# Adding the experts' results to the residual rows in memory by accumulating scatters

## The chip, the core and the metric

The kernel runs on one core of a Trainium2 chip. A core has a matrix engine (TensorE, PE in the profile), a vector engine (VectorE, DVE), a scalar engine (ScalarE, ACT), GpSimd (POOL) and a synchronising engine (SyncE, SP) that here only issues DMAs. Sixteen DMA engines move data between the device's memory and the core's on-chip memory. The metric is the device time of one execution in microseconds; less is better.

## What is computed

One layer of a decoder for 512 tokens of width 1024, all in float32: a norm, an input projection, two parallel token mixers, an output projection with a residual sum, and then a mixture of experts, which takes most of the time. Cut to what matters here:

```python
x = x + mix @ w_out[l]
h = rmsnorm(x, g_ffn[l])
# moe: softmax router, each token goes to the 4 best of 32 experts, gates g
#   expert e: act = clamped_swiglu(h[rows] @ w1[e] + b1[e])   w1[e]: 1024 x 2048
#             y   = act @ w2[e] + b2[e]                       w2[e]: 1024 x 1024
#   out[token] = sum over its 4 experts of g * y
x = x + moe(h, w_router[l], b_router[l], w1[l], b1[l], w2[l], b2[l])
return rmsnorm(x, g_final)
```

Every expert has 12.58 MB of weights, so all 32 have 403 MB, and each is read once.

## The kernel before

The engines run hand-written programs side by side and wait for one another on semaphores. The order of the work is thus the order in the code of each engine.

**Up to the router.** The mixers and the output projection come first. Then, for each of the four blocks of 128 tokens, VectorE writes the residual sum `X` (it stays on chip), `second_norm` makes the rows h, and ScalarE issues two stores of them: into `h2_dram`, which has four rows for each token (2048 rows of 4 KB), one store for the first copy and one for the other three (L1489, L1490). The router picks four experts for each token. VectorE computes where each of the 2048 pairs of token and expert stands in the experts' lists (`list_entries`, L1180). An entry has two numbers: the row 4 x token + k, where k is the rank of the expert among the token's four in order of work, and the gate. GpSimd scatters the entries into `slot_list` in memory (L1708), reads the lists back, and turns row numbers into numbers of half rows and quarter rows.

**Lists.** An expert's block has 64 slots whose rows are handled as two halves (128 lines of 2 KB). The 18 "big" experts have 32 slots more, handled in quarters (128 lines of 1 KB). `KINDS` gives the order of big and small: BBSS and then four times BBSBSBS. A slot without a token holds `UNUSED`, a number beyond the last row; the indirect DMAs have a bound, and a line whose index is beyond it is left out (`oob_is_err=False`).

**The expert stage.** `expert_blocks` calls the same step on each engine for expert i = 0 to 31. SyncE (`load`, L428) streams the weights through a ring of 16 slots of 1 MB: eight slots of w1 for expert i, four of w2 for expert i - 1, each load as soon as TensorE has used the slot (`slot_used`). TensorE (`compute`, L831) does w1 of expert i, turns the gathered rows of expert i + 1, does w2 of expert i - 1. VectorE and ScalarE do the activation, and ScalarE's `gated` (L1522) multiplies the result by the gates into `gated_y`, one of two buffers. GpSimd (`move`, L1724) issues, in this order: the scatter of expert i - 2, the gather of the rows of expert i + 2 once TensorE has turned the block before, and a small copy that selects the biases. The scatter writes gated rows into `expert_rows` (`y_dram`, 2048 rows, every row written once) as halves (L1690) and for a big expert quarters (L1693).

**The end.** As w1 of the last expert is used up, SyncE starts to read `expert_rows` back: rows k = 0, 1, 2 of all tokens, each set as soon as the scatters allow (a row k of some token can come from no expert after 28 + k in the order), and k = 3 after all scatters (`all_scattered`, L1771). VectorE adds each set to `X` (`add_row`, L1274). Then ScalarE squares and sums, VectorE multiplies by the reciprocal root and the gain (`last_norm`), and SyncE stores the output. The branches for overflowing experts are not taken with these inputs.

Of the kernel before, what the change touches and what calls it, by code (L numbers as in the profile page):

```python
# [5 lines left out]
F32 = mybir.dt.float32  # L6
# [4 lines left out]
ALU = mybir.AluOpType  # L11
# [3 lines left out]
P = 128  # L15
# [26 lines left out]
UNUSED = 1 << 20  # L42
ROWS = SEQ * TOPK
# [31 lines left out]
def layer_kernel(nc, x, g_mix, w_in, conv_w, sinks, g_attn_out, g_conv_out, w_out,  # L75
                 g_ffn, w_router, b_router, w1, b1, w2, b2, g_final, out):
    ctx = ExitStack()
    with ctx:
# [89 lines left out]
        first_row = sb("first_row", [P, TB])  # L168
        smaller = sb("smaller", [P, TB, TOPK, TOPK])
# [64 lines left out]
        h2_copies = h2_dram.rearrange("(t p k) n -> t p k n", p=P, k=TOPK)  # L234
# [52 lines left out]
        h2_turned, h2_stored, h2_copied = sem("h2_turned"), sem("h2_stored"), sem("h2_copied")  # L287
# [21 lines left out]
        yrow_in = [[sem(f"yrow{k}_in{t}") for t in range(TB)] for k in range(TOPK)]  # L309
        sum_ready, fstd_ready, fin_ready, out_written = sem("sum_ready"), sem("fstd_ready"), sem("fin_ready"), sem("out_written")  # L310
# [60 lines left out]
        def _(sp):  # L371
# [94 lines left out]
            n_ovf = overflow_count(sp)  # L466
            with sp.If(n_ovf < 1):
# [15 lines left out]
            def finish_overflow():  # L483
                sp.wait_ge(all_scattered, 1)
                for k in range(TOPK - 1):
                    load_row(k)

            overflow_blocks(sp, n_ovf, load_overflow, finish_overflow)

            sp.wait_ge(all_scattered, 1)
            load_row(TOPK - 1)
# [379 lines left out]
        def _(dve):  # L872
# [307 lines left out]
            def list_entries():  # L1180
# [20 lines left out]
                then(v.tensor_copy(row_i[:, :, :], row_f[:, :, :]))  # L1201
# [592 lines left out]
```

## Time and profile before

| | us |
|---|---|
| Median of 3 runs (lowest to highest) | 1254.84 (1253.53 to 1255.98) |
| The profiled execution | 1252.27 |
| its span in the trace | 1250.5 |
| TensorE busy | 1158.2 |
| VectorE busy | 309.7 |
| ScalarE busy | 198.1 |
| GpSimd busy | 169.9 |

The terms of an estimate come from the profiled execution and are summed against its own time; the median of the runs lies 2.6 us above it. Busy times overlap, and matmuls are pipelined, so a large busy time alone doesn't make an engine the bound. The share of the DMA engines and the waits have to be read beside it.

### The profile page before, as it was taken

Reading aid. Unit: us, or ns where it says so; the run is one execution under the profiler, and the core shown is the slowest. Engines: PE = TensorE matmul, PEld = TensorE weight load, DVE = VectorE, ACT = ScalarE, POOL = GpSimd, SP = SyncE. Lnnn points to the kernel's source line nnn. Section 1 sums busy time; section 2 is a strip of 40 time slices with the busy share of each in tenths; the row PEclk is TensorE's granted clock in tenths of the full one; section 3 lists DMA queues with packets and bytes.
Section 4 is the critical chain, followed back from the end, with each engine's and each line's share of the span. In section 5 each row is a group of like instructions: output and inputs, shape, how many; then the busy total and the mean of one; then the engine's idle time right before and its main releaser. Section 6 shows DMA issues by size and latency. Waiting matters only on the chain. (4 is left out here: it accounts for less than half of the span.)

```text
span 1250.5 us, 16597 instructions
## 1 busy us (share of the span) xinstructions
PE 1158.2 (93%) x7030; PEld 484.9 (39%) x7030; DVE 309.7 (25%) x470; ACT 198.1 (16%) x385; POOL 169.9 (14%) x246
## 2 busy tenths in 40 slices
PE   5999998798999999999999898999989899998980
PEld 4777677323333333333333333333333333333330
DVE  4678855411101202101101010110101011010108
ACT  4453623001001101011010000101000010100002
POOL 6000000341111201111111011111101111111000
PEclk9999989698999999999999999999999999999995
DMA  9400635999999999999999999999999999999996
GB/s 332 145 1 27 236 142 220 320 392 411 423 424 424 423 425 423 425 422 425 424 423 425 425 423 424 425 423 423 424 424 424 423 425 423 424 423 424 425 394 249
DMA packets 59246, 460.67 MB, mean 368 GB/s; under 512 B 12438, under 2 KB 12710, under 8 KB 26306
## 3 DMA queue, kind: packets, MB, share of 16 engines
q1 hardware_dynamic: 49362, 434.15, 84.0%
q0 software_dynamic: 7632, 17.05, 3.6%
q10 hardware_dynamic: 2176, 8.39, 1.7%
q8 instruction: 57, 0.93, 0.3%
q14 instruction: 19, 0.16, 0.0%
HBM read 442.58 MB, written 21.41 MB: 371 GB/s over the span
## 5 line engine op out<-in xcount | busy, mean ns | idle before, releaser
L778 PE MATMUL ps<-ring_a,blockT 128*64 128x512 f32 x1472 | 327.2, 595 | 15.6 <-DMA ring_a<-in_w 15.5
L1234 DVE TENSOR_SCALAR xnT<-ps 128x768 f32<-128x768 f32 (+1 forms) x32 | 26.9, 841 | 828.4 <-PE ps L785 520.6
L778 PEld LDWEIGHTS ps<-ring_a,blockT 128*64 128x64 f32 x1472 | 101.1, 137 | 226.8 <-issue 187.7
L804 PE MATMUL ps<-ring_a,actT 128*64 128x512 f32 x736 | 166.3, 598 | 0.0
L1497 ACT ACTIVATE blockT<-ps 128x512 f32<-128x512 f32 x30 | 17.9, 597 | 561.4 <-PE ps L730 561.4
L778 PE MATMUL ps<-ring_b,blockT 128*64 128x512 f32 x448 | 99.7, 595 | 6.7 <-DMA ring_b<-in_w 6.7
L1674 POOL DMA_INDIRECT scores<-h_rows,slots x30 | 31.7, 1058 | 509.6 <-PE ps L730 508.7
L785 PE MATMUL ps<-ring_a,blockT 128*32 128x512 f32 x768 | 87.4, 595 | 0.0
L804 PEld LDWEIGHTS ps<-ring_a,actT 128*64 128x64 f32 x736 | 50.2, 137 | 93.5 <-issue 91.0
L1690 POOL DMA_INDIRECT expert_rows<-normed,slots x32 | 32.9, 1029 | 270.1 <-ACT normed L1526 269.8
L804 PE MATMUL ps<-ring_b,actT 128*64 128x512 f32 x288 | 64.7, 596 | 0.0
L524 PE MATMUL ps<-xnT_hi,ring_r 128*128 128x512 f32 x144 | 57.8, 401 | 5.6 <-DVE ring_r L892 3.5
L778 PEld LDWEIGHTS ps<-ring_b,blockT 128*64 128x64 f32 x448 | 30.7, 137 | 71.0 <-issue 57.3
L525 PE MATMUL ps<-xnT_lo,ring_r 128*128 128x512 f32 x144 | 56.9, 395 | 0.0
L526 PE MATMUL ps<-xnT_hi,ring_r 128*128 128x512 f32 x144 | 56.8, 394 | 0.0
L810 PE MATMUL ps<-ring_a,actT 128*32 128x256 f32 x832 | 50.3, 382 | 0.0
L785 PEld LDWEIGHTS ps<-ring_a,blockT 128*32 128x32 f32 x768 | 22.5, 109 | 62.6 <-issue 62.6
L1255 DVE TENSOR_TENSOR xnT<-xnT 128x768 f32<-128x768 f32 (+1 forms) x32 | 42.7, 1334 | 9.3 <-ACT xnT L1520 8.7
L810 PEld LDWEIGHTS ps<-ring_a,actT 128*32 128x32 f32 x832 | 24.4, 109 | 34.5 <-issue 21.1
L1525 ACT ACTIVATE normed<-ps,slots 128x256 f32<-128x256 f32 x18 | 8.5, 474 | 174.5 <-PE ps L810 174.5
L1526 ACT ACTIVATE normed<-ps,slots 128x512 f32<-128x512 f32 x32 | 21.9, 684 | 81.8 <-PE ps L804 81.8
L804 PEld LDWEIGHTS ps<-ring_b,actT 128*64 128x64 f32 x288 | 20.0, 136 | 35.9 <-issue 35.0
(289 smaller groups left out, 1090.3 us busy)
## 6 DMA issues: line engine op xcount, KB each, us to landing
ring_a<-in_w SPq DMA_DIRECT2D x98, 2048.0 KB, 32.1
ring_a<-in_w SPq DMA_DIRECT2D x92, 1024.0 KB, 30.1
ring_b<-in_w SPq DMA_DIRECT2D x30, 2048.0 KB, 31.0
ring_b<-in_w SPq DMA_DIRECT2D x36, 1024.0 KB, 32.8
ring<-in_w_in SPq DMA_DIRECT2D x12, 768.0 KB, 19.2
ring<-expert_rows SPq DMA_DIRECT2D x16, 512.0 KB, 14.7
h_rows<-normed ACTq DMA_DIRECT2D x4, 1536.0 KB, 6.5
X<-in_x SPq DMA_DIRECT2D x8, 512.0 KB, 6.1
```

The costliest lines, as they stand in the source:

```text
L524: mm(ps[:, bank, :], high[:, k, :], xnT_hi[:, k, :], start=(k == 0), stop=False)
L525: mm(ps[:, bank, :], high[:, k, :], xnT_lo[:, :, k, :], start=False, stop=False)
L526: ins = mm(ps[:, bank, :], low[:, k, :], xnT_hi[:, k, :], start=False, stop=(k == KT - 1))
L778: ins = mm(ps[half * HALF:(half + 1) * HALF, b, :], x_of(k)[0], ring(r)[:, 0, at + half * 512:at + (half + 1) * 512], start=False, stop=(k ...
L785: mm(ps[q * QUARTER:(q + 1) * QUARTER, B_BOTH, :], x_of(k)[1], w[:, :, q * 256:(q + 1) * 256], start=False, stop=(k == KT - 1), tile_posit ...
L804: ins = mm(ps[half * HALF:(half + 1) * HALF, bank, :], actT[:, s % 2 * W2_K + j, s // 2 * HALF:(s // 2 + 1) * HALF], ring(r)[:, 0, j * D + ...
L810: ins = mm(ps[q * QUARTER:(q + 1) * QUARTER, bank + 1, 0:256], actT[:, 4 + j, s * QUARTER:(s + 1) * QUARTER], ring(slot(s)[0])[:, 0, j * D ...
L1234: v.tensor_scalar(width(glu_c, big), width(ps_glu, big), LIMIT, None, ALU.min).then_inc(glu_ready, 1)
L1255: v.tensor_tensor(turned.rearrange("p (s k q) -> p s q k", k=W2_K, q=P), a_in.rearrange("p (s q k) -> p s q k", k=W2_K, q=P), b_in.rearran ...
L1526: a.activation(gated_y[:, parity, 0:512], ps[:, bank, :], ACT.Copy, scale=gates[:, HALVES, 1:2].bitcast(F32)).then_inc(y_ready, 1)
L1674: g.indirect_dma_start(gathered[:, 0:512], None, h2_halves, bass.IndirectOffsetOnAxis(lists[:, HALVES, 0:1], 0), bounds_check=last_half_ro ...
L1690: g.indirect_dma_start(y_halves, bass.IndirectOffsetOnAxis(slots[:, HALVES, i, 0:1], 0), gated_y[:, parity, 0:512], None, bounds_check=las ...
```

## The change

The results are no longer kept as four rows for each token. ScalarE stores the residual rows `X` to memory too (`x2_rows`, 512 rows and 640 spare rows behind them), and every expert's scatter adds its gated rows to them with an accumulating indirect DMA. The sum is read back once, into `X`. From this follow:

- `h2_dram` has one row for each token; one store of 0.5 MB instead of 2 MB, and one of 0.5 MB for `X`.
- An entry names the token instead of 4 x token + k, so the operations that found k go, and `entry` is filled by GpSimd beforehand.
- An unused entry holds 512 + its rank in the list, a spare row of `x2_rows`: the gather still leaves it out, the scatter adds something to a spare row.
- A token may be in the lists of several experts, so a scatter first waits until the scatter of the expert before has landed (`y_out[1 - parity]`).
- At the end 4 reads of 0.5 MB instead of 16, and no additions on VectorE.

```diff
-        h2_dram = nc.dram_tensor("h2_rows", (ROWS, D), F32).ap()
+        h2_dram = nc.dram_tensor("h2_rows", (SEQ, D), F32).ap()
-        y_dram = nc.dram_tensor("expert_rows", (ROWS, D), F32).ap()
+        x2_dram = nc.dram_tensor("x2_rows", (SEQ + LIST_RANKS, D), F32).ap()
...
@@ SyncE, the end
-            y_dram_v = y_dram.rearrange("(t p k) n -> k p t n", p=P, k=TOPK)
-
-            def load_row(k):
-
-                for t in range(TB):
-                    sp.dma_start(y_rows[:, k, t, :], y_dram_v[k][:, t, :]).then_inc(yrow_in[k][t], 16)
...
-                for k in range(TOPK - 1):
-                    sp.wait_ge(slot_used, USES * (w1_slot(E - 1, KT - 1) + 1))
-                    for b in range(2):
-                        sp.wait_ge(y_out[b], scatters(b, E - TOPK + k))
-                    load_row(k)
...
             sp.wait_ge(all_scattered, 1)
-            load_row(TOPK - 1)
+            for t in range(TB):
+                sp.dma_start(X[:, t, :], x2_dram[t * P:(t + 1) * P, :]).then_inc(x_in[t], 16)
...
@@ VectorE, second_norm, list_entries and the end
-                    dve.wait_ge(h2_copied, 16 * t)
...
-                then(v.tensor_copy(row_i[:, :, :], row_f[:, :, :]))
-                then(v.tensor_tensor(picked[:, :, :, :].rearrange("p t k e -> p (t k) e"), onehot[:, :, :, :].rearrange("p t k e -> p (t k) e"),
-                                     by_place.to_broadcast([P, TB * TOPK, E]), ALU.mult))
-                then(v.tensor_reduce(row_f[:, :, :], picked[:, :, :, :], AX_X, ALU.add))
-                then(v.tensor_tensor(smaller[:, :, :, :], row_f[:, :, :].unsqueeze(3).to_broadcast([P, TB, TOPK, TOPK]),
-                                     row_f[:, :, :].unsqueeze(2).to_broadcast([P, TB, TOPK, TOPK]), ALU.is_gt))
-                then(v.tensor_reduce(row_f[:, :, :], smaller[:, :, :, :], AX_X, ALU.add))
-                v.tensor_tensor(entry[:, :, :, 0:1].rearrange("p t k w -> p t (k w)"), row_f[:, :, :], first_row[:, :].unsqueeze(2).to_broadcast([P, TB, TOPK]),
-                                ALU.add).then_inc(entries_ready, 1)
+                v.tensor_copy(row_i[:, :, :], row_f[:, :, :]).then_inc(entries_ready, 1)
...
-            def add_row(k, t):
-                dve.wait_ge(yrow_in[k][t], 16)
-                if k:
-                    dve.wait_ge(sum_ready, (k - 1) * TB + t + 1)
-                v.tensor_tensor(X[:, t, :], X[:, t, :], y_rows[:, k, t, :], ALU.add).then_inc(sum_ready, 1)
...
             for t in range(TB):
-                add_row(TOPK - 1, t)
-                dve.wait_ge(sum_ready, (TOPK - 1) * TB + t + 1)
-                if t:
-                    last_norm(t - 1)
-            last_norm(TB - 1)
+                last_norm(t)
...
@@ ScalarE, the stores and the end
-                act.dma_start(h2_copies[t, :, 0, :], normed[:, t % 2, :]).then_inc(h2_stored, 16)
-                act.dma_start(h2_copies[t, :, 1:TOPK, :], normed[:, t % 2, :].unsqueeze(1).to_broadcast([P, TOPK - 1, D])).then_inc(h2_copied, 16)
+                act.dma_start(h2_dram[t * P:(t + 1) * P, :], normed[:, t % 2, :]).then_inc(h2_stored, 16)
+                act.dma_start(x2_dram[t * P:(t + 1) * P, :], X[:, t, :]).then_inc(x2_stored, 16)
...
-                act.wait_ge(sum_ready, (TOPK - 1) * TB + t + 1)
+                act.wait_ge(x_in[t], 48)
...
@@ GpSimd, the spare rows and the scatters
-            then(g.memset(list_fill, UNUSED))
+            then(g.iota(list_fill.rearrange("p (b e) -> p b e", b=LIST_RANKS // P), [[1, LIST_RANKS // P], [0, 2 * E]], base=SEQ, channel_multiplier=LIST_RANKS // P))
...
+            def add_parts(lists, big, parity, done):
+
+                g.indirect_dma_start(x2_halves, bass.IndirectOffsetOnAxis(lists[:, HALVES, 0:1], 0), gated_y[:, parity, 0:512], None,
+                                     bounds_check=end_halves, oob_is_err=True, compute_op=ALU.add).then_inc(done, 16)
+                if big:
+                    g.indirect_dma_start(x2_quarters, bass.IndirectOffsetOnAxis(lists[:, QUARTERS, 0:1], 0), gated_y[:, parity, 512:768], None,
+                                         bounds_check=end_quarters, oob_is_err=True, compute_op=ALU.add).then_inc(done, 16)
+
             def scatter(i, parity):
                 pool.wait_ge(y_ready, i + 1)
-                g.indirect_dma_start(y_halves, bass.IndirectOffsetOnAxis(slots[:, HALVES, i, 0:1], 0), gated_y[:, parity, 0:512], None,
-                                     bounds_check=last_half_row, oob_is_err=False).then_inc(y_out[parity], 16)
...
+                if i:
+                    pool.wait_ge(y_out[1 - parity], scatters(1 - parity, i - 1))
+                add_parts(slots[:, 0:2, i, :], BIG[i], parity, y_out[parity])
...
-            pool.wait_ge(h2_copied, 16 * TB)
+            pool.wait_ge(x2_stored, 16 * TB)
```

On GpSimd the last scatters stand like this in the kernel before: expert 29, then 30 (two parts), then 31, and the read of the overflow count. `normed` is the buffer of the gated rows.

```order
L1648 COPY bias_sel<-expert_sel 96x128 [waits w2_begun]
L1690 DMA expert_rows<-normed,slots 4096x512 [waits y_ready] x2
L1693 DMA expert_rows<-normed,slots 8192x256
L1690 DMA expert_rows<-normed,slots 4096x512 [waits y_ready]
L358 TENSOR_LOAD ovf_row [waits ovf_in,y_out1,y_out0]
```

And like this in the changed kernel, where `x_rows` is the tensor of the residual rows:

```order
L1594 COPY bias_sel<-expert_sel 96x128 [waits w2_begun]
L1637 DMA x_rows<-normed,slots 2304x512 [waits y_out0,y_ready]
L1637 DMA x_rows<-normed,slots 2304x512 [waits y_out1,y_ready]
L1640 DMA x_rows<-normed,slots 4608x256
L1637 DMA x_rows<-normed,slots 2304x512 [waits y_out0,y_ready]
L352 TENSOR_LOAD ovf_row [waits ovf_in,y_out1,y_out0]
```

The scatters stand where they stood, and each has got a wait for the one before.

On VectorE the end of the kernel before has the last set of additions between the norms:

```order
L1278 TENSOR_TENSOR X<-X,ring 128x1024 x2
L1296 RECIPROCAL stat<-stat 128x1
L1298 SCALAR_TENSOR_TENSOR ring<-X,stat,gain_a 128x1024
L1278 TENSOR_TENSOR X<-X,ring 128x1024
L1296 RECIPROCAL stat<-stat 128x1
L1298 SCALAR_TENSOR_TENSOR ring<-X,stat,gain_a 128x1024
```

In the changed kernel only the norms are left:

```order
L356 UNCONDITIONAL_BRANCH
L1245 RECIPROCAL stat<-stat 128x1
L1247 SCALAR_TENSOR_TENSOR ring<-X,stat,gain_a 128x1024
L1245 RECIPROCAL stat<-stat 128x1
L1247 SCALAR_TENSOR_TENSOR ring<-X,stat,gain_a 128x1024
```

The four additions here and the twelve of the other sets ahead of them are gone.

## Rows read from the trace of the kernel before

**Rows 1.** The page: busy us (share) xinstructions; DMA busy in tenths, 40 slices of the span.

```profile
PE 1158.2 (93%) x7030; PEld 484.9 (39%) x7030; DVE 309.7 (25%) x470; ACT 198.1 (16%) x385; POOL 169.9 (14%) x246
...
DMA  9400635999999999999999999999999999999996
```

**Rows 2.** Stretches: us, busy us (instructions) of PE, PEld, DVE, ACT, POOL; PE clock, DMA share, GB/s.

```profile
235.00:300.00 65.00, 58.08 (x356) 18.83 (x356) 12.41 (x19) 5.20 (x8) 21.98 (x27) 0.92 1.01 391
...
385.00:594.00 209.00, 209.00 (x1338) 71.46 (x1336) 26.66 (x32) 20.93 (x41) 31.23 (x31) 1.00 1.01 424
594.00:812.00 218.00, 210.28 (x1334) 70.70 (x1332) 26.67 (x32) 20.87 (x40) 29.59 (x29) 1.00 1.01 424
```

**Rows 3.** Timeline of ScalarE: start us, us; sigmoids of three experts, each seven apart.

```profile
407.38 0.83 ACT L1520 ACTIVATE xnT<-xnT 128x768 f32<-128x768 f32 x1
...
615.88 0.83 ACT L1520 ACTIVATE xnT<-xnT 128x768 f32<-128x768 f32 x1
...
833.78 0.84 ACT L1520 ACTIVATE xnT<-xnT 128x768 f32<-128x768 f32 x1
```

**Rows 4.** Waits, whole span: engine line <- releaser: us in total, times, longest.

```profile
POOL scores L1674 <- PE ps L730: 508.7, 29, 21.9
...
PEld ps L778 <- DMA ring_a<-in_w: 36.8, 31, 2.7
...
DVE stat L1078 <- ACT stat L1322: 5.0, 4, 1.5
```

**Rows 5.** DMA issues: count, KB each, median us from issue to landing.

```profile
ring_a<-in_w SPq DMA_DIRECT2D x98, 2048.0 KB, 32.1
```

**Rows 6.** DMA queue of GpSimd, whole span: packets, MB, share of 16 engines.

```profile
q0 software_dynamic: 7632, 17.05, 3.6%
```

**Rows 7.** DMA queues from 300 to 1200 us: SyncE's, with the weights, and GpSimd's.

```profile
q1 hardware_dynamic: 33421, 364.94, 96.3%
q0 software_dynamic: 6288, 15.34, 4.4%
```

**Rows 8.** Timeline of the tail: start us, us, instruction, idle before it and its releaser.

```profile
1198.05 3.65 PE L778 MATMUL ps<-ring_a,blockT 128*64 128x512 f32 x16 [1.06 <-DMA ring_a<-in_w]
...
1216.82 0.98 POOL L1693 DMA_INDIRECT expert_rows<-normed,slots  x1 [0.30 <-issue]
...
1237.60 1.06 ACT L1568 ACTIVATE ring<-X 128x1024 f32<-128x1024 f32 x1 [13.39 <-DVE X L1278]
...
1238.98 1.04 ACT L1568 ACTIVATE ring<-X 128x1024 f32<-128x1024 f32 x1
```

**Rows 9.** The chain that ended last: start us, us, what.

```profile
1222.76 1.20 DMA expert_rows<-normed,slots
1223.96 6.05 issue
...
1231.38 4.88 DMA ring<-expert_rows
...
1246.19 1.29 DVE ring L1298
```

**Rows 10.** Scatters of halves (L1690), all 32, from issue to landing.

```profile
DMA to landing us min/median/max: 5.5/7.9/10.0
```

**Rows 11.** Timeline of GpSimd: two scatters and the gather between them.

```profile
331.27 1.03 POOL L1690 DMA_INDIRECT expert_rows<-normed,slots  x1 [9.95 <-ACT normed L1526]
...
345.75 1.06 POOL L1674 DMA_INDIRECT scores<-h_rows,slots  x1 [12.14 <-PE ps L730]
...
353.72 1.03 POOL L1690 DMA_INDIRECT expert_rows<-normed,slots  x1 [4.58 <-ACT normed L1526]
```

**Rows 12.** Timeline between the router and the first expert.

```profile
227.32 1.09 POOL L1683 DMA_INDIRECT scores<-h_rows,tok_static  x1 [74.34 <-DVE tok_static L1146]
...
236.81 0.69 DVE L1202 TENSOR_TENSOR scores<-scores,where 128x512 f32<-128x512 f32 x1
...
239.87 1.04 POOL L1708 DMA_INDIRECT slot_list<-entry,row_i  x1 [5.42 <-DVE entry L1208]
```

More of the change, by code:

```diff
@@ L41 @@
 NEG = -1e30
-UNUSED = 1 << 20
-ROWS = SEQ * TOPK
 LIST_BLOCKS = SEQ // P
@@ L307, in layer_kernel @@
         all_scattered = sem("all_scattered")
-        yrow_in = [[sem(f"yrow{k}_in{t}") for t in range(TB)] for k in range(TOPK)]
-        sum_ready, fstd_ready, fin_ready, out_written = sem("sum_ready"), sem("fstd_ready"), sem("fin_ready"), sem("out_written")
+        fstd_ready, fin_ready, out_written = sem("fstd_ready"), sem("fin_ready"), sem("out_written")
         dve_final, act_final = sem("dve_final"), sem("act_final")
@@ L481, in load_overflow @@
                     load_w2(e, k, KT + k)
[L483 to L488, printed above, removed]
+            overflow_blocks(sp, overflow_count(sp), load_overflow)
             sp.wait_ge(all_scattered, 1)
-            load_row(TOPK - 1)
+            for t in range(TB):
+                sp.dma_start(X[:, t, :], x2_dram[t * P:(t + 1) * P, :]).then_inc(x_in[t], 16)
             for t in range(TB):
@@ L1266, in _ @@
             expert_blocks(elementwise)
-            def add_rows():
-                for k in range(TOPK - 1):
-                    for t in range(TB):
-                        add_row(k, t)
-            def add_row(k, t):
-                dve.wait_ge(yrow_in[k][t], 16)
-                if k:
-                    dve.wait_ge(sum_ready, (k - 1) * TB + t + 1)
-                v.tensor_tensor(X[:, t, :], X[:, t, :], y_rows[:, k, t, :], ALU.add).then_inc(sum_ready, 1)
-            n_ovf = overflow_count(dve)
-            with dve.If(n_ovf < 1):
-                add_rows()
             def overflow(o, i):
@@ L1287, in overflow @@
                 activated(i, True)
-            overflow_blocks(dve, n_ovf, overflow, add_rows)
+            overflow_blocks(dve, overflow_count(dve), overflow)
             dve.wait_ge(gfinal_in, 16)
@@ L1619, in _ @@
             g.iota(iota_o[:, :], [[0, 1]], base=0, channel_multiplier=1, allow_small_or_imprecise_dtypes=True)
-            g.iota(first_row[:, :], [[P * TOPK, TB]], base=0, channel_multiplier=TOPK, allow_small_or_imprecise_dtypes=True)
-            g.iota(tok_value[:, :, 0:1], [[0, TB], [0, 1]], base=0, channel_multiplier=TOPK, allow_small_or_imprecise_dtypes=True)
-            g.iota(tok_value[:, :, 1:2], [[P * TOPK, TB], [0, 1]], base=-16384, channel_multiplier=0, allow_small_or_imprecise_dtypes=True)
+            for t in range(TB):
+                g.iota(entry[:, t, :, 0:1], [[0, TOPK], [0, 1]], base=t * P, channel_multiplier=1)
+            g.iota(tok_value[:, :, 0:1], [[0, TB], [0, 1]], base=0, channel_multiplier=1, allow_small_or_imprecise_dtypes=True)
+            g.iota(tok_value[:, :, 1:2], [[P, TB], [0, 1]], base=-16384, channel_multiplier=0, allow_small_or_imprecise_dtypes=True)
             g.iota(expert_no[:, :], [[0, 1]], base=0, channel_multiplier=1, allow_small_or_imprecise_dtypes=True)
@@ L1661, in _ @@
             g.iota(iota_r[:, 0:HALF].rearrange("p (a b) -> p a b", b=8), [[1, 8], [8, 8]], base=-1024, channel_multiplier=0, allow_small_or_imprecise_dtypes=True).then_inc(consts_ready, 1)
-            last_row = pool.to_reg(ROWS - 1)
-            last_half_row = pool.to_reg(2 * ROWS - 1)
-            last_quarter_row = pool.to_reg(4 * ROWS - 1)
+            last_row = pool.to_reg(SEQ - 1)
+            last_half_row = pool.to_reg(2 * SEQ - 1)
+            last_quarter_row = pool.to_reg(4 * SEQ - 1)
             h2_halves = h2_dram.rearrange("t (h n) -> (t h) n", h=2)
             h2_quarters = h2_dram.rearrange("t (h n) -> (t h) n", h=4)
-            y_halves = y_dram.rearrange("t (h n) -> (t h) n", h=2)
-            y_quarters = y_dram.rearrange("t (h n) -> (t h) n", h=4)
+            x2_halves = x2_dram.rearrange("t (h n) -> (t h) n", h=2)
+            x2_quarters = x2_dram.rearrange("t (h n) -> (t h) n", h=4)
+            end_halves, end_quarters = (pool.to_reg(n * (SEQ + LIST_RANKS) - 1) for n in (2, 4))
             list_rows = list_dram.rearrange("(r e) w -> r (e w)", e=E)
```

15 lines of the change are left out of this document (2 added, 13 removed).

## The prediction

> **What bounds the kernel now.** I read the share of each engine first [rows 1]: TensorE is busy 93% of the span, which looks like the bound. The same page has the 16 DMA engines at 9 tenths or more in 32 of the 33 slices from the eighth on [rows 1]. Two resources are nearly full, so the question is which one sets the pace. The table by stretches [rows 2] shows DMA at 1.01 of its time and 424 GB/s from 385 us to 812 us, whatever TensorE does. TensorE is busy without a gap from 385 to 594 us, then 210.3 of 218 us. The sigmoids, seven experts apart [rows 3], give the two periods: 615.88 - 407.38 = 208.5 us while TensorE still lives on weights that were loaded ahead, then 833.78 - 615.88 = 217.9 us once that lead is used up. So TensorE needs 29.8 us for an expert and DMA 31.1 us. A check from bytes: seven experts are 7 x 12.58 MB of weights plus 7/32 of 16.78 MB gathered and scattered, 91.8 MB; at 424 GB/s that is 216 us, the measured period. TensorE's waits for weights are short and many [rows 4], and a weight load takes some 30 us to land although 2 MB at 424 GB/s need 5 [rows 5]: the queue always holds most of the ring. Hence **DMA is the bound from about 235 us to about 1198 us**, and every microsecond of DMA engine time added there is a microsecond of span.
>
> After the last w1 tile lands (TensorE resumes with it at 1198.05 us [rows 8]) comes a tail without slack: TensorE's last products, the last scatter, the read of the last of four row sets, the final norm [rows 8, 9].
>
> **1. The scatters: bytes.** Before, list entries without a token lie outside the bounds and move nothing. The software queue shows it: 17.05 MB [rows 6] are two times 8.39 MB (2048 rows of 4 KB, gathered and scattered) and 0.27 MB of lists. The gathers stay so. The scatters do not: an unused entry now names a spare row behind the 512 tokens, so all lines move. A big expert moves 128 x 2 KB + 128 x 1 KB = 393 KB, a small one 262 KB; 18 big and 14 small make 10.75 MB instead of 8.39. Before the last w1 load has landed experts 0 to 29 are scattered: 17 x 0.393 + 13 x 0.262 = 10.09 MB now, against 30/32 x 8.39 = 7.86 MB before.
>
> **2. The scatters: price.** Between 300 and 1200 us the software queue moved 15.34 MB in 4.4% of 16 engines' 900 us, 39.6 us: 387 GB/s; the weights' queue 364.94 MB in 866.7 us, 421 GB/s [rows 7]. The old scatters cost 7.86 / 387 = 20.3 us. No row shows an accumulating DMA. The lower bound is what a plain scatter of its bytes costs: 10.09 / 387 = 26.1 us, **+5.8 us**. The upper is a gather and a scatter of its bytes, since it must fetch the old row as a gather does and pass the new one as a scatter does: 52.1 us, **+31.8 us**. I take the upper, because the nearest rows say that an engine's time goes by what it takes in: gathers, scatters and weights, of either direction, all add up to one 1.01 and one 424 GB/s [rows 2, 7], so a second operand that has to be taken in should not be free. A gain is excluded here: more bytes, and nothing is taken from this stage.
>
> The Trainium skill, in "Collectives: The Full Stack", section "The bandwidth ceiling: the fold count and why AG ≠ RS ≠ AR", says of the sum in a DMA engine that the addition itself costs nothing but that it needs two reads on the same ring, and that this halves the rate. By that rule the step is the upper value, +31.8 us; without it, from 1.01 of plain copies alone, the lower, +5.8 us, can't be excluded. No run here shows it yet.
>
> **3. The new wait.** Each scatter now waits on GpSimd for the one before it to land. Queued behind it are the gather of rows for the next-but-one expert and the copy of the bias selector. Scatters land in a median of 7.9 us, at most 10.0 [rows 10]; the closest two are 22.4 us apart (331.27 and 353.72), and the gather behind them waits another 14.5 us for TensorE (345.75) [rows 11]. In all, GpSimd waits 508.7 us for TensorE before its gathers [rows 4]. Cost 0, as long as landing stays under 22 us; beyond some 30 us it would starve TensorE of rows.
>
> **4. The stored copies of h.** Instead of 2 MB per 128 tokens, 0.5 MB of h and 0.5 MB of x. All of it stands before 235 us. VectorE's second norm, which also waits for the copies, was released by ScalarE all four times [rows 4]. The last store competes with weights at 216 us, but the first gather is issued at 227.32 us, released by VectorE's static list and not by a store [rows 12]. Gain 0, at most 0.5 us.
>
> **5. Five VectorE operations fewer for the list.** The first starts at 236.81 us, and GpSimd's first list scatter, which waits for the last, at 239.87: 3.1 us, of which the 0.9 of a release stay, so about 2 [rows 12]. The first indexed gather comes earlier by that. But DMA is at 1.01 in this stretch too [rows 2], so TensorE only gains lead. Worth 0. If TensorE were the bound it would be worth 2 us.
>
> **6. The tail.** Fewer row reads (6 MB less, two thirds of them beside TensorE's last products), no additions, one more wait.
> - Scatter 30's second part is issued at 1216.82 [rows 8]. With a landing of some 7.4 us (a little under the median of all, since the row reads that competed are gone) plus 1 to 2 us for the accumulation it lands at about 1225.5; scatter 31, which started at 1222.76, starts 2.7 us later. It needed 7.25 us to 1230.01 [rows 9]; in an emptier queue the smallest landing of all is 5.5 us [rows 10], plus 1 to 2 for the accumulation, so 7 again. SP is released at about 1234 instead of 1231.38: +2.6 us.
> - Before, from there: 4.88 us to the first row's landing, then for each 128 tokens an addition and a norm on VectorE; the last norm ends at 1246.19 + 1.29 = 1247.48, 16.1 us after the issue [rows 9]. Now ScalarE squares what landed: 4.9 us, four steps of 1.38 us (1238.98 - 1237.60 [rows 8]), the last root 0.3, reciprocal 0.2, norm 1.29 [rows 9], gaps 0.1: 12.4 us. The gain is 3.7 us; the 3.0 us of the last store stay.
> - Sum of the tail: -3.7 + 2.6 = **-1.1 us**. At best (landing 5.5 us twice, no wait) -5.6 us; at worst, with landings of 12 us, +7 us.
>
> **Sum.** The profiled execution took 1252.27 us (span 1250.5). 1252.27 + 31.8 - 1.1 = 1283.0 us. It lies 2.6 us under the median of the runs, 1254.84, on which the same sum gives 1285.5; I say **1285 us**. A measurement of this kernel can tell some 0.2% (2.5 us) from no change.
>
> **Rivals.**
> - *One pass.* The old row is fetched beside the other traffic and only the extra lines cost: +5.8 - 1.1, 1259.5 us; half way to the forecast 1272. For it: reading and writing could overlap in an engine. Against: traffic of both directions did not make the mixed queues faster than weights alone.
> - *Faster: the weight stream is not touched and the tail is shorter.* Place: the last 30 us. If an engine adds in the shade of the packets of weights, steps 1 and 2 cost 0 and the best tail holds: 1254.84 - 5.6 = 1249 us. It decides when the added DMA time of 30 scatters is below about 1 us. Against: 1.01 busy everywhere [rows 2] and 2.2 MB more, 5.3 us at 424 GB/s.
> - *Accumulation is slower than its bytes.* Each line of 1 or 2 KB waits in the engine for its old value. At twice my price, 104.2 - 20.3 - 1.1 = +82.8, 1338 us; above 22 us of landing the wait of step 3 joins in. For it: lines are small and nothing in the trace shows such a DMA. Against: a landing of 7.9 us for 8 or 16 lines per engine beside a queue of weights shows that plain lines at least are handled one behind another without stalls.
> - *No difference:* price near 1 pass and the best tail: 1254.84 + 5.8 - 5.6 = 1255 us.
>
> **Chances.** Forecast (1275 to 1297): 0.50. One pass or between (1257.5 to 1275): 0.22. Slower than its bytes (above 1297): 0.18, half of it below 1322. Within 0.2%: 0.06. Faster: 0.04. A range of 1258 to 1322 leaves out the last two, the other half of the third, and little else: 2 in 10. Slower 0.90, same 0.06, faster 0.04.
>
> **What would show it.** Right: seven experts take about 225 us (218 + 7 x 31.8/30) with DMA still at 1.01; TensorE's waits for w1 in the ring's first part grow from 36.8 us [rows 4] to above 55; the software queue's share rises from 3.6% [rows 6] to about 6%; scatters land in 9 to 13 us; the last norm ends 12 us after SP's first read. Wrong: a period of 218 to 219.5 us (one pass or none); landings above 20 us with GpSimd waiting for the scatter before (the slow rival); DMA share below 1 with TensorE without gaps, which would mean that the bound was misread.

## The result, and the profile after

| | before | changed |
|---|---|---|
| Median of 4 runs each, us | 1255.41 | 1273.86 |
| lowest to highest | 1253.53 to 1257.28 | 1272.39 to 1276.39 |
| Profiled execution / its span | 1252.27 / 1250.5 | 1274.83 / 1273.0 |
| Ratio, 95% interval | | 1.0149, 1.0134 to 1.0164 |

The change costs 18.5 us, 1.5%. The forecast was 30, with 1258 to 1322 as the range: right in sign and cause, and too large by 12 us.

The queues from 300 to 1200 us (packets, MB, share of 16 engines), of the changed kernel, answer to [rows 7]:

```profile
q1 hardware_dynamic: 32298, 353.10, 93.2%
q0 software_dynamic: 9696, 17.22, 8.2%
```

GpSimd's queue takes 8.2% of the engines' time instead of 4.4%, 34 us more in 900, while its bytes rose only from 15.34 to 17.22 MB. The weights' queue still moves 421 GB/s while it is served, but it is served 93.2% of the time and not 96.3%, so in the same 900 us it has delivered 12 MB less, nearly an expert's weights. The 3.1% that the weights' queue lost are 28 us. The bytes counted for the whole span show that the old value that an accumulating line fetches isn't counted:

```profile
q0 software_dynamic: 11408, 19.40, 6.7%
```

19.40 MB are 8.39 (gathers) + 10.75 (all lines) + 0.27 (lists). Against [rows 6] this is the 2.36 MB of unused lines and nothing else.

The sigmoids of the same three experts as in [rows 3], and that of the last expert, in ScalarE's timeline of the changed kernel:

```profile
409.37 0.83 ACT L1465 ACTIVATE xnT<-xnT 128x768 f32<-128x768 f32 x1
...
625.62 0.84 ACT L1465 ACTIVATE xnT<-xnT 128x768 f32<-128x768 f32 x1
...
850.83 0.83 ACT L1465 ACTIVATE xnT<-xnT 128x768 f32<-128x768 f32 x1
...
1231.63 0.63 ACT L1465 ACTIVATE xnT<-xnT 128x512 f32<-128x512 f32 x1 [18.76 <-DVE xnT L1199]
```

Seven experts take 850.83 - 625.62 = 225.2 us where they took 217.9. In the seven before them the lead of loaded weights ran out earlier: 216.3 us instead of 208.5. The last sigmoid is a good mark between stream and tail, since everything behind it is bound to the end and not to the weights: in nine of the fourteen traces of this document the last scatter starts 20.25 us after it, whatever the kernel. In the kernel before it stood here:

```profile
1202.50 0.63 ACT L1520 ACTIVATE xnT<-xnT 128x512 f32<-128x512 f32 x1 [17.33 <-DVE xnT L1234]
```

So in this pair of traces the stream got 29.1 us longer, and the tail behind the mark went from 1250.5 - 1202.5 = 48.0 to 1273.0 - 1231.6 = 41.4 us. TensorE's waits for weights say the same (compare the first with [rows 4]; columns us in total, times, longest):

```profile
PEld ps L752 <- DMA ring_a<-in_w: 57.4, 40, 3.4
...
PEld ps L752 <- DMA ring_b<-in_w: 18.7, 12, 3.4
...
POOL x_rows L1637 <- DMA x_rows<-normed,slots: 5.2, 1, 5.2
```

The last of these rows is the new wait: of 31 scatters that could have waited for the one before, one did, the last (in e6's trace below, with the same wait, none did). An accumulating scatter of halves lands later in the stream than a plain one in [rows 10], and sooner at the end:

```profile
L1637 POOL DMA_INDIRECT x_rows<-normed,slots x32: 1571/1629/1657, 306.1 to 1253.3; - x32
...
DMA to landing us min/median/max: 4.8/11.6/12.6
```

The first row also shows GpSimd needing 1.63 us to issue one, where the plain one took 1.03 [rows 11].

The end of the chain (start us, us, what), against [rows 9]:

```profile
1253.29 1.57 DMA x_rows<-normed,slots
1254.86 3.35 issue
...
1259.26 3.40 DMA X<-x_rows
...
1268.63 1.28 DVE ring L1247
```

From the last scatter's start to SP's read it takes 5.97 us (8.62 before), from there to the end of the last norm 10.65 us (16.1 before).

### The profile page after: what moved, and what is told of

The parts are those of the page before. It is cut to its first block and busy times, and to the rows that moved or that the text cites. A ratio compares the mean times of both kernels' runs of the same rounds, so it can differ in the third digit from the quotient of the medians.

```text
span 1273.0 us, 16579 instructions
## 1 busy us (share of the span) xinstructions
PE 1171.3 (92%) x7030; PEld 484.6 (38%) x7030; DVE 287.6 (23%) x449; ACT 197.8 (16%) x385; POOL 200.6 (16%) x249
## 3 DMA queue, kind: packets, MB, share of 16 engines
q0 software_dynamic: 11408, 19.40, 6.7%
HBM read 436.29 MB, written 17.22 MB: 356 GB/s over the span
## 5 line engine op out<-in xcount | busy, mean ns | idle before, releaser
L752 PE MATMUL ps<-ring_a,blockT 128*64 128x512 f32 x1472 | 336.6, 606 | 26.3 <-DMA ring_a<-in_w 25.7
L752 PE MATMUL ps<-ring_b,blockT 128*64 128x512 f32 x448 | 103.9, 613 | 9.4 <-DMA ring_b<-in_w 9.2
L1637 POOL DMA_INDIRECT x_rows<-normed,slots x32 | 51.8, 1618 | 271.8 <-ACT normed L1471 266.3
L759 PEld LDWEIGHTS ps<-ring_a,blockT 128*32 128x32 f32 x768 | 22.5, 109 | 62.6 <-issue 62.6
```

What stands on the lines that cost most here:

```text
L752: ins = mm(ps[half * HALF:(half + 1) * HALF, b, :], x_of(k)[0], ring(r)[:, 0, at + half * 512:at + (half + 1) * 512], start=False, stop=(k ...
L759: mm(ps[q * QUARTER:(q + 1) * QUARTER, B_BOTH, :], x_of(k)[1], w[:, :, q * 256:(q + 1) * 256], start=False, stop=(k == KT - 1), tile_posit ...
L1637: g.indirect_dma_start(x2_halves, bass.IndirectOffsetOnAxis(lists[:, HALVES, 0:1], 0), gated_y[:, parity, 0:512], None, bounds_check=end_h ...
```

## The experiments

Below, "stream" is the time of the last sigmoid in the profiled execution, "tail" the span behind it. "From expert 3" is the part of the stream behind the sigmoid of expert 3: that sigmoid stands anywhere from 344.7 to 349.9 us in the fourteen traces, without order by kernel (346.27 and 349.87 us in the two of the kernel before), and this is no effect of the scatters. Medians are of runs beside runs of the kernel before on the same chip, and each ratio is against those: their medians were 1256.04 us for e1 to e4, 1254.16 us for e5 to e8 and 1255.93 us for e9 to e12.

| kernel | median, us | ratio (95%) | stream | from expert 3 | tail |
|---|---|---|---|---|---|
| before | 1255.41 | 1 | 1202.5 | 856.2 | 48.0 |
| changed | 1273.86 | 1.0149 (1.0134 to 1.0164) | 1231.6 | 883.4 | 41.4 |
| e1 plain, all lines | 1248.33 | 0.9946 (0.9931 to 0.9960) | 1207.7 | 859.2 | 38.4 |
| e2 adding, used lines | 1268.30 | 1.0092 (1.0077 to 1.0107) | 1226.1 | 877.9 | 40.3 |
| e3 plain, used lines | 1244.22 | 0.9903 (0.9889 to 0.9917) | 1203.4 | 857.2 | 38.4 |
| e4 adding, half width | 1248.91 | 0.9938 (0.9925 to 0.9950) | 1206.0 | 860.6 | 38.0 |
| e5 three reads back | 1283.38 | 1.0214 (1.0187 to 1.0242) | 1234.2 | 885.0 | 48.7 |
| e6 four additions back | 1276.01 | 1.0176 (1.0150 to 1.0202) | 1229.7 | 884.3 | 44.0 |
| e7 two sums, no wait | 1274.13 (one run) | | 1232.2 | 884.8 | 40.1 |
| e8 before again | 1258.06 (one run) | | 1207.6 | 857.7 | 48.6 |
| e9 gather beside scatter | 1267.61 | 1.0089 (1.0071 to 1.0107) | 1225.6 | 879.8 | 38.4 |
| e10 before, slots spread | 1252.01 | 0.9970 (0.9958 to 0.9982) | 1200.5 | 853.9 | 47.7 |
| e11 e2, slots spread | 1260.41 | 1.0040 (1.0026 to 1.0054) | 1218.0 | 873.3 | 39.9 |
| e12 copies of h back | 1274.21 | 1.0145 (1.0124 to 1.0166) | 1230.8 | 885.2 | 40.6 |

### e1, e2, e3: addition and unused lines, each alone

```diff
@@ e1 and e3 (both calls in add_parts)
-                                     bounds_check=end_halves, oob_is_err=True, compute_op=ALU.add).then_inc(done, 16)
+                                     bounds_check=end_halves, oob_is_err=True).then_inc(done, 16)
@@ e2 and e3
-                                     bounds_check=end_halves, oob_is_err=True
+                                     bounds_check=last_half_row, oob_is_err=False
... (the quarters likewise)
```

> The changed kernel with a plain indirect write in place of the accumulating one; all lines are still moved, the unused ones into the spare rows. The sum over experts is left out (the last writer of a row stands). Theory A (an accumulating line costs an engine two passes, a plain one a single pass): the scatters of experts 0 to 29 cost 26 us instead of 50 to 52, so the last w1 load lands 5 to 6 us later than in the kernel before, the tail is about 6 us shorter as in the changed kernel, and the time is that of the kernel before within 2 us, some 19 us under the changed one. Theory B (the stretch comes from the spare lines or from the wait for the scatter before, not from the addition): 1268 to 1274 us, as in the changed kernel. Landing of a scatter: A 8 to 9 us, B 12 us.

> The changed kernel with the unused lines left out of the accumulating scatters by the bound, as in the kernel before; the addition stays. Theory A (time goes by bytes, two passes each): 7.86 MB twice at 387 GB/s are 40.6 us against 20.3 before, so the last w1 load lands 20 us later than before and 9 us earlier than in the changed kernel: about 1264 us. Theory B (the lines cost, whether they carry a used slot or not): no difference from the changed kernel, 1272 to 1275 us.

> The changed kernel with plain writes and with unused lines left out: the scatters' traffic is that of the kernel before, and only the new end (one set of rows read, no additions), the smaller stores and the shorter list are left of the change. The sum over experts is left out. Theory A: the last w1 load lands as in the kernel before within 1.5 us, and the whole gain of the tail shows, 5 to 7 us under the kernel before: 1249 to 1250 us. Theory B (the tail gains 1 us, as the working of the prediction had it): 1254 us.

With plain writes the whole loss is gone, and e1 is 7 us under the kernel before; with the unused lines left out too, what is left of the change is a gain of 12 us (e3). e3's stream is that of the kernel before (from expert 3, 857.2 us against 856.2 and 857.7); its tail is 9.6 us shorter. The addition costs 24.1 us on the used lines (e2 less e3), of which 1.9 in the tail. The unused lines cost 4.1 us by the medians and 5.4 by the ratios when written plainly (e1 less e3), and 5.6 or 7.2 when added (changed less e2): under the 5.8 and well under the 11.5 us that one and two passes over 2.23 MB would take. e2 itself came out 4 us above what theory A had for it. e1 came out some 7 us and e3 5 us under their figures; 3 to 4 us of that are the tail, which gained more than I had put in, and the rest was not traced. The bytes set the sign and the rough size, and something else a part of it; e10 and e11 ask for that.

### e4: bytes or lines

```diff
-        x2_dram = nc.dram_tensor("x2_rows", (SEQ + LIST_RANKS, D), F32).ap()
+        x2_dram = nc.dram_tensor("x2_rows", (SEQ + LIST_RANKS, D // 2), F32).ap()
... (the store of x and the last read take half the columns too)
@@ add_parts: the halves; the quarters, [:, parity, 512:768], become [:, parity, 512:640]
-gated_y[:, parity, 0:512], None,
+gated_y[:, parity, 0:256], None,
```

> The changed kernel with residual rows of half the width: every accumulating line carries half its bytes (1 KB and 512 B), with the same number of lines. The right half of the columns is left out of the experts' sum, and the last read is half as long. Theory A (price by bytes): half of the scatters' 52 us stays, 26 us, so 5 to 6 us above the kernel before in the stream, and 7 to 9 us less in the tail: 1251 to 1255 us. Theory B (price by lines, each waiting for its old value): nearly the whole 29 us of the stream stays, less some 2 us in the tail: 1268 to 1272 us.

1248.9 us, 2 us under theory A's range and far from theory B's. With as many accumulating lines of half the length the stream ends at 1206.0 us, next to e1's 1207.7: two passes of half lines against one pass of full ones, the same number of bytes. Halving the bytes took the stream's excess over e3 from some 27 us to 3.4 (from expert 3), since half of two passes is the one that e3 pays too. The price goes by bytes, two passes of them; a line that waits in the engine for its old value is ruled out as the main term. The queue's row of e4 from 300 to 1200 us, and that of e1:

```profile
q0 software_dynamic: 9840, 12.44, 5.8%
```

```profile
q0 software_dynamic: 6294, 17.48, 4.9%
```

The share is a little larger in e4 though the stream isn't longer, so the share of an accumulating queue reads high: what it adds to the busy time is not all taken from the weights.

### e9: is an addition a gather and a scatter?

```diff
             def scatter(i, parity):
                 pool.wait_ge(y_ready, i + 1)
+                if i < E - 2:
+                    read_old(i)
...
@@ read_old (halves; quarters likewise; each expert's waits for the one before)
+                g.indirect_dma_start(upper[:, 0:512], None, h2_halves, bass.IndirectOffsetOnAxis(slots[:, HALVES, i, 0:1], 0),
+                                     bounds_check=last_half_row, oob_is_err=False).then_inc(old_in, 16)
```

> The kernel of e3 (plain scatters of the used lines, new end, the sum over experts left out), and for experts 0 to 29 a plain gather of the same lines (of h, into a spare tile) is issued just ahead of the scatter. That is what step 2 of the prediction took an accumulating scatter to be. Theory A (the price of the addition is the pass that fetches the old row): 7.86 MB at 387 GB/s, +20 us on e3's 1244.2 us, 1264 us, which is e2 (1268.3 us) less 2 us of its longer tail and within 3 us. Theory B (an accumulating line costs more than a gather and a scatter): 1254 to 1260 us. Theory C (it costs less): above 1268 us.

1267.61 us, +23.4 us on e3; e2, with the addition, +24.1 us. The streams end at 1225.6 and 1226.1 us. Of the 1.9 us by which e2's tail is longer, 1.6 lie between the start of its last scatter and SP's read (5.92 us against 4.33), and 0.3 in that read. The figure of theory A was 3.6 us too low, because a pass cost 23.4 us and not 20 (e10 and e11 are about that), but its comparison with e2 holds. That is the prediction's price of step 2 shown directly: for the weight stream, an accumulating scatter costs what a gather and a scatter of its lines cost, within 1 to 2 us of 23 (from expert 3, e9 is 1.9 us longer than e2).

### e5, e6, e7: the tail

```diff
@@ e5, SyncE, where the kernel before had its reads
+            for k in range(TOPK - 1):
+                sp.wait_ge(slot_used, USES * (w1_slot(E - 1, KT - 1) + 1))
+                for b in range(2):
+                    sp.wait_ge(y_out[b], scatters(b, E - TOPK + k))
+                for t in range(TB):
+                    sp.dma_start(y_rows[:, k + 1, t, :], old_v[k][:, t, :]).then_inc(yrow_in[k][t], 16)
@@ e6, VectorE
+                v.tensor_tensor(X[:, t, :], X[:, t, :], gain_a[:, :], ALU.add).then_inc(sum_ready, 1)
@@ e7, GpSimd (and a second tensor, x2_odd, for odd experts)
-                if i:
-                    pool.wait_ge(y_out[1 - parity], scatters(1 - parity, i - 1))
+                if i >= 2:
+                    pool.wait_ge(y_out[parity], scatters(parity, i - 2))
```

> The changed kernel, and beside it the three further sets of 2 MB are read at the end at the points where the kernel before read rows k = 0, 1, 2 (from other memory; nothing is added from them, so the result is the changed kernel's). Theory A (the tail got shorter because nothing competes with the last scatter and the last read): from the start of the last scatter to SP's release it takes 8 to 9 us again instead of 6.0, the last scatter also starts some 1 to 3 us later since the one before lands later, and the time rises by 4 to 7 us. Theory B (the reads were hidden beside TensorE's last products anyway, as the prediction had it for two thirds of them): at most 2 us.

> The changed kernel with one VectorE addition of 128x1024 put back for each block of tokens between the last read and the norm, as in the kernel before. What is added is a constant tile, so the output is off by it. Theory A (additions and norms take turns on VectorE, 2.7 us for a block instead of 1.4): the end of the last norm comes 4 to 5 us after that of the changed kernel, +4 to +5 us. Theory B (the reads set the pace and additions hide in it): +1.5 us.

> The changed kernel with two tensors for the sum, one for even and one for odd experts, so that no scatter waits for the one before it (only for the one before that). The odd tensor is left out of the final sum. Theory A (in the stream the wait costs nothing, in the tail it costs what the landing of scatter 30 takes): w1's last tile is used within 1.5 us of the changed kernel's time, the last scatter starts 24.7 us after that instead of 26.1. Theory B (the wait holds GpSimd and the gathers behind it): the stream gets 10 us shorter or more.

The tail falls into four parts, us, from the profiled executions:

| kernel | mark to start of last scatter | to SP's read | to its first landing | to the end | tail |
|---|---|---|---|---|---|
| before | 20.3 | 8.6 | 4.9 | 14.2 | 48.0 |
| e8 before again | 20.5 | 9.0 | 4.9 | 14.2 | 48.6 |
| e3 plain, used lines | 20.3 | 4.4 | 3.4 | 10.3 | 38.4 |
| changed | 21.7 | 6.0 | 3.4 | 10.3 | 41.4 |
| e12 copies of h back | 21.0 | 5.9 | 3.4 | 10.3 | 40.6 |
| e5 three reads back | 24.7 | 10.3 | 3.4 | 10.3 | 48.7 |
| e6 four additions back | 20.3 | 6.1 | 3.4 | 14.3 | 44.0 |
| e7 two sums, no wait | 20.3 | 5.9 | 3.5 | 10.3 | 40.1 |

e5's tail is 48.7 us, 7.3 more than the changed kernel's. GpSimd's timeline shows where the first part goes:

```profile
1249.09 1.56 POOL L1653 DMA_INDIRECT x_rows<-normed,slots  x1 [0.30 <-issue]
1258.88 1.57 POOL L1650 DMA_INDIRECT x_rows<-normed,slots  x1 [8.23 <-DMA x_rows<-normed,slots]
```

The last scatter waits 8.23 us for the one before (5.18 in the changed kernel), and the chain shows the second part: it lands late, beside the third set, whose reads land from 1263.60 to 1269.26 us.

```profile
1258.88 1.57 DMA x_rows<-normed,slots
1260.45 7.69 issue
...
1269.20 3.39 DMA X<-x_rows
```

10.3 us from its start to SP's read instead of 6.0. Theory A holds, above its upper figure by the medians (+0.65%, 8 us). In the changed kernel such reads would be paid twice, in the wait for the scatter before and in the last landing. The kernel before has no such wait, and its last scatter starts 20.3 us after the mark like e3's. Its price for the reads is read against e3, whose end is this:

```profile
1223.62 0.98 DMA x_rows<-normed,slots
...
1228.01 3.44 DMA X<-x_rows
```

From the last scatter's start to SP's read e3 takes 4.4 us, the kernel before 8.6, and its first read 4.9 instead of 3.4, since three of its third set's reads land only after that read is issued (at 1232.47 to 1234.98 us, against 1231.38). So there the reads cost 5.7 us. They were not hidden. e5 doesn't repeat the slower first read: there the third set has landed when it starts.

e6's tail is only 2.6 us longer than the changed kernel's, but its last scatter happened to start 1.4 us earlier after the mark, as the table shows. Behind the first landing it takes 14.3 us instead of 10.3, 3.9 us more, and the last norm ends 14.6 us after SP's read instead of 10.65: the 4 to 5 us of theory A, at their lower end (by the ratios the time rises by 3.4 us). The kernel before has the same 14.2 us. The start of e6's chain, and four pieces from it that show VectorE's norm of one block followed at once by the addition of a later one:

```profile
1249.94 1.57 DMA x_rows<-normed,slots
...
1256.03 3.42 DMA X<-x_rows
...
1265.22 1.29 DVE ring L1248
1266.51 1.15 DVE X L1253
...
1267.68 1.16 ACT ring L1519 x2
...
1269.39 1.28 DVE ring L1248
```

e7's stream ends at 1232.2 us, as the changed kernel's within 0.6, and its tail is 1.3 us shorter. Here the last scatter starts when ScalarE has written its rows:

```profile
1252.47 1.57 POOL L1640 DMA_INDIRECT x_odd<-normed,slots  x1 [3.78 <-ACT normed L1472]
```

That is 24.7 us after the last w1 tile is used, theory A's figure. So the wait costs nothing in the stream. At the end it cost 1.4 us in the changed kernel's trace, 0.7 in e12's and nothing in e6's, which all have it. Between e3 and the kernel before the pieces close: 38.4 us, with 5.7 for the reads and 3.9 for the additions, are 48.0. The changed kernel keeps of that 1.4 us of wait and 1.6 us of slower landing.

### e8: the kernel before, a second time

> The kernel before, unchanged, profiled a second time, since its first profiled execution lay 2.6 us under the median of its runs. Theory A (what varies between its executions is the tail, where its row reads and the last scatter compete): the last w1 tile is used within 1 us of 1198 us and the rest takes 1 to 4 us longer than 52.4 us. Theory B (the weight stream varies): the last w1 tile comes 1 to 4 us later, the tail takes 52 to 53 us.

The tail is nearly the same (48.6 us), the stream ends 5.1 us later: theory B, a little above its figures. Most of the 5.1 us stands already in the first experts, while TensorE still has its lead. The sigmoid of expert 2, in the first and the second trace (e8):

```profile
318.93 0.62 ACT L1520 ACTIVATE xnT<-xnT 128x512 f32<-128x512 f32 x1
```

```profile
322.53 0.62 ACT L1520 ACTIVATE xnT<-xnT 128x512 f32<-128x512 f32 x1
```

3.6 us of 5.1. The two traces lie on either side of the kernel's median (1252.27 and 1258.06 against 1255.41 us), and the changed kernel's 1.0 us above its own, which is why the pair of profiles shows 22.5 us where the medians show 18.5. What varies there was not looked into.

### e12: the stores of h

```diff
+                act.dma_start(h2_more.rearrange("(t p k) n -> t p k n", p=P, k=TOPK - 1)[t], normed[:, t % 2, :].unsqueeze(1).to_broadcast([P, TOPK - 1, D])).then_inc(x2_stored, 16)
@@ GpSimd
-            pool.wait_ge(x2_stored, 16 * TB)
+            pool.wait_ge(x2_stored, 32 * TB)
@@ VectorE, second_norm
+                    dve.wait_ge(x2_stored, 32 * t)
```

> The changed kernel with the three further copies of h stored again for each block of tokens (into a tensor that nobody reads), and with the waits on them where they were. Theory A (step 4 of the prediction: all this lies before the weight stream is the bound): within 1 us of the changed kernel, 1272 to 1275 us. Theory B (6.3 MB less to store is a gain hidden in the total): 1277 us or more, and the first w1 product of expert 0 starts 2 us later or more.

No difference (ratios 1.0145 and 1.0149): 6.3 MB of stores ahead of the stream are free.

### e10, e11: where the unused lines stand

```diff
@@ list_entries
-                v.tensor_scalar(eighths.bitcast(I32), moved.bitcast(I32), 3, None, ALU.logical_shift_right)
+                v.tensor_scalar(eighths.bitcast(I32), moved.bitcast(I32), 4, None, ALU.logical_shift_right)
...
-                v.scalar_tensor_tensor(out=eighths, in0=moved, scalar=-9.0, in1=ranks[:, :, :], op0=ALU.mult, op1=ALU.add)
+                v.scalar_tensor_tensor(out=eighths, in0=moved, scalar=-21.0, in1=ranks[:, :, :], op0=ALU.mult, op1=ALU.add)
...
-                then(v.scalar_tensor_tensor(out=moved, in0=moved, scalar=7.0, in1=ranks[:, :, :], op0=ALU.mult, op1=ALU.add))
+                then(v.scalar_tensor_tensor(out=moved, in0=moved, scalar=3.0, in1=ranks[:, :, :], op0=ALU.mult, op1=ALU.add))
```

The quarters and the two lists that are made ahead (`iota_r`) follow in the same way; four lines more.

> The kernel before, with another order of the slots within a block: rank r of a list goes to line 4r - 63 floor(r/16) of the halves instead of 8r - 63 floor(r/8), and likewise in the quarters, so that used lines are spread over groups of four neighbouring lines from the first 16 ranks on. Reason: in e1, e2, e3 and the changed kernel the unused lines cost 4.1 us when written plainly and about 5 us when accumulated, where their bytes at 387 GB/s would be 5.8 and 11.5 us. 
> The kernel of e2 (accumulating scatters of the used lines only) with the slot order of e10. Theory A: gathers once and accumulating scatters twice, so 3 x 48 KB x 16 at 387 GB/s, 6 us under e2's 1268.3: 1262 us. Theory B: as e2. In both, still some 7 us or more above the kernel before, since the second pass remains.

Both came as theory A has it: the kernel before gains 3.9 us (ratio 0.9970, 0.9958 to 0.9982; 4 expected), e2 gains 7.9 us by the medians and 6.5 by the ratios (6 expected). Neither moves a byte more or less, as the rows for 300 to 1200 us show, e10's first, with 15.34 MB as in [rows 7], and e11's 15.15 MB, which e2 has too:

```profile
q0 software_dynamic: 6288, 15.34, 4.4%
```

```profile
q0 software_dynamic: 9696, 15.15, 6.9%
```

So where the left-out lines stand counts, and not the bytes alone. That it is the fullest group of lines that sets the cost is what theory A says; both sizes agree with it, but no row shows a single DMA engine, and the new order also changes the order in which rows of memory are visited; the two were not separated. e10 leaves nothing of the computation out and is faster than both kernels. e11 is the best form of the accumulating scatters found here, and still 0.4% slower than the kernel before: the second pass outweighs the tail.

## Why the prediction was right, and where it was off

**The bound.** Right. DMA was at 1.02 of its time in the changed kernel and the added pass lengthened the period of seven experts. The forecast period was 225 us, the measured one 225.2.

**Step 1, bytes.** Right for the queue (19.40 MB). Wrong as a measure of the old price: 7.86 MB with lines left out did not cost 7.86 MB. Theory A of e10 and e11 counts lines by the DMA engine that moves them; by the counts of these inputs the fullest engine then carried 588 KB in each direction where the mean was 512 and all lines are 656. (The assignment of lines to engines is that of the Trainium skill, "DMA: Bandwidth & Descriptors", "The descriptor swizzle"; e10 and e11 bear it out by their effect, and no trace here shows it.) For 30 of 32 scatters that is 9.0 MB worth, 23.3 us, and by this estimate the change adds 28.8 instead of 31.8 us. The same count gives e9 less e3 as 23.3 us (measured 23.4), e2 less e3 as 23.3 + 1.9 (24.1), and the changed kernel less e2 as 5.5 (5.6).

**Step 2, price.** The mechanism and the end of the range that was taken were right: e9 equals e2, e4 excludes a price by lines, e1 fits one pass. The Trainium skill's rule on reductions ("Collectives: The Full Stack", "The bandwidth ceiling: the fold count and why AG ≠ RS ≠ AR"), that the addition is free and the second read is not, agrees with e2, e4 and e9. One caution goes with it: the queue's own busy share overstates the loss, 34 us of share against some 27 us of stream (and 28 us of share that the weights' queue lost).

**The stream's total.** The changed kernel and its four relatives with the same scatters (e5, e6, e7, e12) end their streams at 1229.7 to 1234.2 us, 1231.7 on average; the kernel before at 1202.5 and 1207.6. That is 27 us with an uncertainty of some 3, against 31.8. Counted from expert 3, where the spread between executions falls out, it is 883.4 to 885.2 us against 856.2 and 857.7: 27.6 us. The corrected count explains 3.0 of the difference. Where the rest is was not tested. The sigmoids of experts 3 to 8 stand 2.0 us later in this pair of traces, all alike, but in e6 and e12, which have the same scatters, they stand up to 0.9 us earlier than before, so that shift says nothing on the scatters.

**Step 3, the wait.** Right for the stream: nothing (e7). The closest two scatters are 22.4 us apart only there; in the tail scatter 31 starts 5.9 us behind the second part of scatter 30 (1216.82 and 1222.76 [rows 8, 9]), and there the wait costs 0 to 1.4 us, for which step 6 has a term.

**Step 4, stores.** Right, 0 (e12).

**Step 5, the list.** Right that it gains nothing, wrong on the way. GpSimd's first list scatter starts 2.0 us earlier, as said:

```profile
237.83 1.03 POOL L1661 DMA_INDIRECT slot_list<-entry,row_i  x1 [3.29 <-DVE row_i L1174]
...
280.22 1.15 POOL L1621 DMA_INDIRECT scores<-h_rows,slots  x1 [0.92 <-POOL slots L1672]
```

but the first indexed gather at 280.22 us is no earlier than before (279.85): GpSimd waited longer for the lists to land behind the weights, so in this pair not even a lead for TensorE came of it. In e9 and e12, with the same shorter list, that gather is issued at 279.08 and 278.58 us.

**Step 6, the tail.** This is the term that was mis-sized: -1.1 us forecast, -6.6 us in this pair, -7 against both traces of before, beyond the -5.6 that step 6 gave as its best case. The working failed in one thing three times over: it used landings out of a crowded queue where the queue was now nearly empty. Scatter 30's second part was given 8.7 us to land and took 6.0, so that scatter 31, which was to start 2.7 us later, started 1.4 us later after the mark. Scatter 31 was given 7 us and took 4.8. The first read was given 4.9 us and took 3.4. "Two thirds of them beside TensorE's last products" was true of the clock and wrong as a price: in the kernel before these reads cost 5.7 us, by delaying the last scatter and the first read of the fourth set, and put back into the changed kernel they cost 7.3 (e5). The additions were sized right: 3.7 us in the working, 3.9 in e6.

**The rivals.** One pass is excluded by e1 against the changed kernel, and the slower one by e4. The faster rival had the tail half right: e3, whose stream is untouched, is at 1244 us, 5 us better than that rival's figure. It failed at its point of decision, the added DMA time.

Of the 12 us between forecast and result, the tail accounts for some 6 and the stream for the rest, of which 3 by the count of lines. Both errors have the same sign. The result lies 1 us under the forecast's own band (1275 to 1297) and in the one given to "one pass or between", though two passes are what happened: the cause was forecast better than the size. Of the signs, the period (225.2 us), the waits for w1 (57.4 us), the queue's share (6.7%) and the landings (11.6 us) came as said; the last norm ended 10.65 us after SP's first read and not 12.

## What to carry to other kernels

Where DMA is the bound, price an accumulating scatter as a gather plus a scatter of its bytes, and compare it with what the separate read back costs: at the end of a kernel, reads that seem hidden beside compute can still hold up the last small transfers on which the end hangs. When indirect DMAs leave lines out, try spreading the used ones over groups of neighbouring lines: counting bytes was not enough here. That the fullest group sets the cost is the reading that fits e10 and e11, and not a shown fact. And split the time at a mark that both kernels share, into stream and tail, before explaining a total: here some +27 and -7 hid behind one +18.5 (the two come from single traces, hence the 1.5 us left over).

## What the runs showed that I had not expected

- The order of slots within a block was worth 0.3% on a tuned kernel, with the same bytes and as many instructions (e10), and 0.5 to 0.6% with accumulating scatters (e11).
- In the stream an accumulating scatter of halves landed in 11.6 us (plain 8.1 in e1), and at the end, in a nearly empty queue, in 4.8 (plain 3.3 in e3). GpSimd took 1.63 us instead of 1.03 to issue it.
- The three row reads beside the last scatters cost more (5.7 us in the kernel before, 7.3 in the changed one) than the four additions on the path (3.9 us).
